# Turning the activations of block 2 before the first projection unit, with its loads, squares and splits reordered

## What is computed

```python
h = rmsnorm(x, norm_mix)                      # x: 512 + 32 rows of 1024
q_a, k_a, v_a, q_g, k_g, v_g, r_g, f_lr, gate_a, gate_b = split(h @ w_in)
a_out = window_attention(rope(q_a), rope(k_a), v_a, sinks)
g_out, state = gated_linear_attention(q_g, k_g, v_g, f_lr, r_g, state)
merged = sigmoid(gate_a) * (a_out @ w_proj_attn) + sigmoid(gate_b) * (g_out @ w_proj_gla)
x = x + merged @ w_out
x = x + moe(rmsnorm(x, norm_ffn))             # 32 experts, top 2 within the top group
y = rmsnorm(x, norm_final)
```

## Time and profile before

| | us |
|---|---|
| median of 3 runs | 819.06 |
| lowest and highest | 818.98, 821.65 |
| the profiled execution | 818.98 |
| its span | 817.1 |
| PE busy in the span | 728.4 |
| DVE busy | 341.2 |
| ACT busy | 244.3 |

### The profile page before, as it was taken

The page is one execution under the profiler, slowest core; times in us unless marked ns, Lnnn a source line. Parts: engine busy times, 40 slices in busy tenths (PEclk is TensorE's granted clock), DMA queues, the critical chain, the costliest instruction groups (busy, mean ns, idle before and its releaser), DMA issues.

```text
span 817.1 us, 12277 instructions
## 1 busy us (share of the span) xinstructions
PE 728.4 (89%) x5112; PEld 541.1 (66%) x5112; DVE 341.2 (42%) x623; ACT 244.3 (30%) x489; POOL 82.9 (10%) x138
## 2 busy tenths in 40 slices
PE   5999999999999998999999999999978879787830
PEld 3889997778999997779999978864433323232310
DVE  6643367754555345244354523732223111111118
ACT  6234284553445432333123232311110101010113
POOL 3404000000001001000000011211112111121200
PEclk9999999999999998999999999999999999898975
DMA  8632111125112614323133299759999999999835
GB/s 315 216 105 61 52 52 52 53 61 147 52 53 71 265 53 173 137 67 102 51 104 93 84 360 380 272 203 397 421 424 422 425 422 421 424 412 399 325 125 221
DMA packets 73415, 173.02 MB, mean 212 GB/s; under 512 B 7040, under 2 KB 41184, under 8 KB 65152
## 3 DMA queue, kind: packets, MB, share of 16 engines
q1 hardware_dynamic: 63520, 148.52, 48.2%
q0 software_dynamic: 9840, 23.72, 7.9%
HBM read 163.26 MB, written 18.74 MB: 223 GB/s over the span
## 4 chain that ended last, share of the span: by engine, by line
PE 63%; DMA 21%; DVE 9%; issue 3%; ACT 2%; SPq 1%; POOL 0%; POOLq 0%; ACTq 0%; DVEq 0%
PE bank L722 41%; DMA expert_down<-in_w_exp_down 16%; PE bank L1187 5%; PE bank L1171 4%; DMA expert_gate_up<-in_w_exp_up 2%; ACT w_split L1225 1%; DVE w_split L1530 1%; DVE s_state L1828 1%; PE bank L742 1%; PE bank L1099 1%; PE bank L1007 1%; PE bank L1013 1%; DVE token_out L2091 1%; SPq L544 1%; DVE token_out L2089 1%
## 5 line engine op out<-in xcount | busy, mean ns | idle before, releaser
L722 PE MATMUL bank<-hT_split,w_split 128*128 128x272 f32 x1152 | 154.1, 292 | 0.0
L722 PEld LDWEIGHTS bank<-hT_split,w_split 128*128 128x128 f32 x1152 | 147.3, 188 | 2.1 <-issue 0.9
L722 PE MATMUL bank<-w_split,hT_split 128*128 128x512 f32 (+1 forms) x576 | 132.3, 384 | 0.7 <-DVE w_split L1530 0.7
L722 PEld LDWEIGHTS bank<-w_split,hT_split 128*128 128x128 f32 x576 | 101.6, 191 | 23.2 <-issue 3.1
L1171 PE MATMUL bank<-expert_gate_up,gatheredT 128*64 128x512 f32 x512 | 112.9, 593 | 3.6 <-DMA expert_gate_up<-in_w_exp_up 2.7
L1530 DVE TENSOR_TENSOR w_split<-w_raw,w_split 128x2048 fp32r<-128x2048 f32 (+1 forms) x35 | 75.9, 2168 | 87.0 <-ACT w_split L1225 87.0
L1187 PE MATMUL bank<-expert_down,expert_actT 128*64 128x512 f32 x256 | 71.8, 712 | 33.5 <-DMA expert_down<-in_w_exp_down 29.6
L1171 PEld LDWEIGHTS bank<-expert_gate_up,gatheredT 128*64 128x64 f32 x512 | 39.1, 137 | 73.8 <-issue 70.1
L1225 ACT ACTIVATE w_split<-w_raw 128x2048 fp32r<-128x2048 f32 (+1 forms) x35 | 63.4, 1812 | 47.9 <-PE bank L722 23.4
L1187 PEld LDWEIGHTS bank<-expert_down,expert_actT 128*64 128x64 f32 x256 | 21.5, 160 | 73.0 <-issue 41.3
L722 PE MATMUL bank<-gla_outT_split,w_split 128*128 128x272 f32 x384 | 49.4, 288 | 0.0
(11 more groups left out here) (355 smaller groups left out, 841.2 us busy)
## 6 DMA issues: line engine op xcount, KB each, us to landing
expert_gate_up<-in_w_exp_gate SPq DMA_DIRECT2D x32, 1024.0 KB, 18.8
expert_gate_up<-in_w_exp_up SPq DMA_DIRECT2D x32, 1024.0 KB, 20.7
expert_down<-in_w_exp_down SPq DMA_DIRECT2D x32, 1024.0 KB, 20.1
w_raw<-in_w_in SPq DMA_DIRECT2D x15, 1024.0 KB, 5.5
w_raw<-in_w_in SPq DMA_DIRECT2D x16, 512.0 KB, 4.7
s_state<-in_state_gla POOLq DMA_DIRECT2D x4, 1024.0 KB, 9.6
out_sample_gla_state<-s_state POOLq DMA_DIRECT2D x4, 1024.0 KB, 6.0
w_raw<-in_w_proj_gla SPq DMA_DIRECT2D x8, 512.0 KB, 4.3
```

The source lines that it names most:

```text
L722: ins = mm(out, stat(x, k), mov(y, k), start=first and n == 0 and m == 0, stop=last and n == len(ks) - 1 and m == 2)
```

## The change

Five edits, all of order; no operation is added, dropped or resized. SP issues the rows of blocks 2 and 3 ahead of the weights of unit 0. PE turns block 2 before unit 0, so that within unit 0 only block 3 is turned, between blocks 0 and 1. ACT squares block 2 before the first copies, and block 3 before `ht_hi(1)`; `split_hi(0)` comes after `ht_hi(1)`. DVE does `norm_h(2)`, `ht_lo(1)` and `norm_h(3)` before `split_lo(0)`, and `ht_lo(3)` before `split_lo(1)`.

```diff
--- before.py
+++ after.py
@@ -506,7 +506,8 @@
             load_x(0)
             sp.dma_start(NMIX[:], a["norm_mix"].partition_broadcast(128).rearrange("p a n -> p (a n)")).then_inc(norm_in, 16)
             sp.dma_start(CF[:, 0:128], a["tables"][:, 0:128]).then_inc(ident_in, 16)
-            load_x(1)
+            for bl in (1, 2, 3):
+                load_x(bl)
 
             def load_unit(u):
                 for dst, src in unit_loads(u):
@@ -521,9 +522,6 @@
 
             for u in range(NU - 2):
                 next_unit(u)
-                if u == 0:
-                    load_x(2)
-                    load_x(3)
                 if u == 1:
                     sp.dma_start(CF[:, 128:NCONST], a["tables"][:, 128:NCONST]).then_inc(tables_in, 16)
             sp.wait_ge(main_mm, unit_done(OUT_UNIT - 1))
@@ -779,8 +777,8 @@
                     if u == 0 and s == 4:
                         pe.wait_ge(h4_out, 2)
                     elif u == 0:
-                        if s in (1, 2):
-                            turn_h(s + 1)
+                        if s == 1:
+                            turn_h(3)
                         pe.wait_ge(h_lo, 2 * POS[s] + 2)
                 elif kind == "kv":
                     pe.wait_ge(q_roped, POS[s] + 1)
@@ -861,7 +859,7 @@
                     ins.then_inc(h_turned, 1)
 
             pe.wait_ge(ident_in, 16)
-            for bl in (4, 0, 1):
+            for bl in (4, 0, 1, 2):
                 turn_h(bl)
 
             def side_pe(step):
@@ -1233,14 +1231,13 @@
                         A(HT4[:, 4 * q:4 * q + 4, :], turned, ACT.Copy).then_inc(h4_out, 1)
                     A(HT[:, 0, 4 * q:4 * q + 4, 128 * bl:128 * bl + n], turned, ACT.Copy).then_inc(h_hi, 1)
 
-            for bl in (4, 0, 1):
+            for bl in (4, 0, 1, 2):
                 square_x(bl)
             ht_hi(4)
             ht_hi(0)
+            square_x(3)
+            ht_hi(1)
             split_hi(0)
-            square_x(2)
-            ht_hi(1)
-            square_x(3)
             ht_hi(2)
             split_hi(1)
             ht_hi(3)
@@ -1552,13 +1549,13 @@
             ht_lo(4)
             norm_h(1)
             ht_lo(0)
-            split_lo(0)
             norm_h(2)
             ht_lo(1)
             norm_h(3)
+            split_lo(0)
             ht_lo(2)
+            ht_lo(3)
             split_lo(1)
-            ht_lo(3)
 
             def rotate(bl, nh, src, dst):
```

## The result

The changed kernel takes 823.55 us (median of 8 runs, 821.34 to 825.32), the kernel before 819.02 in the same comparison (8 runs, 817.91 to 821.65). The ratio is 1.0051 with an interval of 1.0037 to 1.0065. The profiled execution of the changed kernel took 824.56 us (span 822.7), against 818.98 (span 817.1) of before. Forecast were 822.8, in a range from 821.2 to 825.3. In the changed code L722, L742 and L859 have become L720, L740 and L857, `split_lo` L1527 and ACT's `split_hi` L1223.

What follows compares the result with a forecast made beforehand. PE was taken as the bound from 16.97 us on, after a head relayed through ACT, DVE and PE. A start 4.56 us later less 0.87 for the turn gives +3.69 on 819.06, so 822.8 us, range 821.2 to 825.3.

Steps and rivals of the forecast that it cites:

- the sum: Head of the kernel: 4.56 us later start of unit 0 less 0.87 for the turn, +3.69 us in all.
- The turn: PE between token blocks 0 and 1 of unit 0: block 2's turn leaves the bound path, −0.87 us.
- The covers: Head: later weight loads, POOL's loads, block 2's turn and the sample step are hidden in waits and cost nothing.
- the forecast's own spread: Whole kernel: the forecast case without a rival, +3.2 to +4.4 us, given a chance of 0.46.
- the slow-array rival: PE at the start of unit 0: array still at 1.2 GHz, adding 1.7 us, 824.5 in all; chance 0.36.
- The bound from rows: Slow array's price, from sixteen matmuls taking 5.35 us after a wait against 3.65 without: 1.70, taken as 1.2 to 2.3.
- The delay is not swallowed: Denies the rival that DMA waits in the expert stage absorb the head's 3.69 us, giving 819.1; chance 0.09.
- The faster case: Head: `split_lo(0)` still ends by 16.9, so only the turn's 0.87 us counts, 818.2; chance 0.03.
- Late first weights: Loads in each other's way: first weights land after ScalarE asks; at 17.6 adds 0.3 to 0.4, 823.2; chance 0.06.
- the two chances: Whole kernel: slower by more than 0.5% got 0.51, within 0.5% got 0.47, divided at 823.16 us.

Runs made afterwards that it cites:

- The loads with one square alone: Kernel before with x blocks 2 and 3 loaded ahead of the first weights and `square_x(2)` ahead of ACT's first copies: 820.79 us, ratio 1.0016.
- the loads alone: Kernel before with only the loads of x blocks 2 and 3 moved ahead of the first weights on SP: 822.78 us against 820.20, ratio 1.0033.
- the pair with the middle filled: Kernel before and changed kernel, each with nine unread matmuls in the wait near 320 us: 817.84 and 821.66 us, ratios 0.9969 and 1.0021 to plain before.

## Why the prediction was right

**The start.** The order did what the sum says. `split_lo(0)` starts at 18.98 without a wait for ScalarE (forecast 19.18), unit 0 at 21.32 and 21.23 (21.53), after idleness that DVE ends. The 0.2 to 0.3 us missing are an earlier landing of x block 1, not a wrong price: where it landed as in before (the changed kernel with eight filler matmuls) unit 0 started at 21.54. The loads with one square alone gave +1.14 of it.

**The turn.** −0.89 and −0.88 in the two traces, against −0.87. One turn is left among the first 24 matmuls of unit 0.

**The covers.** The weights landed at 13.7 (estimate 13.9), asked for at 16.44. POOL's first transfer went out at 11.48 (11.6). The sample step ended at 20.37 (20.3). That the cover over the weights is needed was shown by the loads alone, which cost ScalarE 1.14 us of waiting without the square.

**The sum.** +3.39 in the execution with an array at full rate, against +3.69. The medians gave +4.5 and +3.7 over before, and +3.8 in the pair with the middle filled. The +4.5 lies just above the forecast's own spread of +3.2 to +4.4; that the range holds it owes something to the slow-array rival. It also leans on a low median of before: 819.02 in 8 runs, but 819.63, 820.02 and 820.20 in the 17, 31 and 29 runs of the later comparisons.

**The slow array.** It got 0.36 as a rival and turned up with 1.4 us or more in three of the four traces of this head (5.19, 4.46 and 4.94 us against 3.04; the fourth had 3.05), so a chance above one half would have fitted better. The bound from rows, 1.2 to 2.3, held for this head: +1.42 to +2.15 (+2.45 with the loads alone). The prediction asked whether the array rises by 21.53 and named an idle wait of 1.2 us in front. The traces say that the idleness doesn't decide it. Where the sample step took 1.81 us or less, so that the array had risen within it, the twelve took 3.04 to 3.07 us, even behind 1.21 us of idleness, or 1.47 in the kernel before with sixteen filler matmuls. Where the sample step took the full 1.93 or 1.94, they took 3.91 to 5.49, with one exception of 3.08 (loads and one square). The Trainium skill (TensorE: Matmul & The Clock Gate, "Part 1: The HAM clock gate") says that the moment of the rise differs between runs of one kernel. The prediction found no run that showed this, and these four traces do.

**The other rivals.** The delay is not swallowed: +5.61 at 36 us is +5.59 at 320 us and, the slow stretches apart, the same within 0.1 us at the end, although PE waits for DMA in the expert stage. The faster case is excluded by the start. Late first weights were seen only where nothing covered them, in the kernel with the loads alone.

**What the prediction didn't have** is the slow stretches at 320 us and in the last pair of experts. They move single executions by 1.4 and 1.7 us, as much as the whole slow-array rival. The 3.43 us wait was in the trace of before, and its 0.50 clock too, but the prediction took its price for a slow array from 606 us and did not ask what such places do to the spread. Such stretches, and the landing of x block 1 (8.57 to 10.28 us in the traces here), are what the traces show of the spread of 4 us between runs of one kernel. How they share it isn't shown: with the stretch at 320 us filled, the kernel before still spread over 4.1 us. The 823.16 that the two chances divide at lies 0.4 us below one median of the changed kernel and 0.15 below the other, less than these runs can tell. That the measured medians fell above it owes as much to luck as to the head.

**What stays open** is how much the slow start adds to the median. The traces have it at 1.4 to 2.2 us in three of four executions, but the medians lie only 0.3 to 1.1 above the +3.39 of the execution without it. Profiled executions may draw it more often than others, or the 4 us spread hides it; no run here tells which. Also open is what makes the array rise within the sample step in one execution and not in the next.

## What to carry to other kernels

A transposition that is hidden in a wait still brings its norm, its square and its copies to the engines whose in-order lists end that wait: here 0.87 us saved on PE cost 4.35 us on ACT and DVE. Count the list of each preparing engine up to the operation that releases the bound engine, before counting what the bound engine saves. And look in the trace for a wait of PE with a granted clock of 0.50 behind it: nine matmuls without use in such a wait made this kernel 0.3% faster, with nothing else changed.

## What the runs showed of the hardware

- The granted clock prints 1.00 in the first 45 us of a plain kernel, while eight turn matmuls take 1.97 us there and 1.03 later. With some filler ahead of them the records of the same stretch print 0.50 to 0.55, and the turns take the same 1.97. At the start of this program the durations tell the clock, the records do not.
- After the filler at the start ended at 7.6 us, PE worked in pieces with gaps of 0.6 to 1.5 us. The first eight small transpositions took 0.65 us (1.03 without filler), but from 12.5 us on the array was at the lower level again.
- The landing of the first loads differs from one execution to the next by up to 1.7 us: x block 1's square started between 8.57 and 10.28 us in the fourteen traces, the first norm on DVE between 7.00 and 8.16.
- Idleness of 0.99 to 1.47 us did not bring the array down once it had risen: twelve matmuls of 512 columns behind it took 3.04 and 3.05 us. They took up to 5.49 us where the work ahead of the wait had still run at the lower level (sample step 1.94 instead of 1.08).
- After the 3.43 us wait the array was slow in each execution without the filler, for 3.5 to 7 us, and in none with it.
